# Two more weight units of the second tile loaded ahead of the expert gather, and TensorE one step further behind

## The reference

```
u = expert_u[idx]; v = expert_v[idx]           # 128 experts for each token, 1024 values each
act = gelu(einsum("td,ted->te", x, u))
y = einsum("te,ted->td", gate * act, v)
```

## Time and profile before

| | |
|---|---|
| median of 3 runs | 1198.71 us (1197.43 to 1200.72) |
| profiled execution | 1200.98 us, span 1199.2 us |
| TensorE busy | 881.1 us (73%) |
| VectorE busy | 815.8 us (68%) |
| ScalarE busy | 256.3 us (21%) |
| POOL busy | 319.6 us (27%) |
| moved by DMA | 402.51 MB, mean 336 GB/s |
| of it gathers and modulation chunks, queue q0 | 293.62 MB |
| of it weights and inputs, queue q1 | 105.62 MB |

### The profile page before, as it was taken

The page is one execution under the profiler, slowest core; times in us unless marked ns, Lnnn a source line. Parts: engine busy times, 40 slices in busy tenths (PEclk is TensorE's granted clock), DMA queues, the critical chain, the costliest instruction groups (busy, mean ns, idle before and its releaser), DMA issues. The chain is left out here.

```text
span 1199.2 us, 17385 instructions
## 1 busy us (share of the span) xinstructions
PE 881.1 (73%) x6808; PEld 667.9 (56%) x6808; DVE 815.8 (68%) x2091; ACT 256.3 (21%) x530; POOL 319.6 (27%) x284
## 2 busy tenths in 40 slices
PE   6999999886786895868444444444445499999998
PEld 6899697875675672745121111211212198888887
DVE  5666555687898767756798777777765689953411
ACT  2411111135222223121021011111100324143100
POOL 0001000142243333414555454544444100000000
PEclk9899999997898797987555555555556699999999
DMA  9977696799999999999999999999999845313230
GB/s 354 393 276 312 246 393 264 272 421 423 403 417 422 415 422 421 422 420 381 421 421 421 421 421 421 421 421 422 419 416 421 333 180 181 117 71 140 107 141 36
DMA packets 51554, 402.51 MB, mean 336 GB/s; under 512 B 5648, under 2 KB 7952, under 8 KB 9104
## 3 DMA queue, kind: packets, MB, share of 16 engines
q0 software_dynamic: 40320, 293.62, 59.7%
q1 hardware_dynamic: 10288, 105.62, 22.1%
q10 hardware_dynamic: 864, 2.16, 0.5%
HBM read 400.32 MB, written 1.05 MB: 335 GB/s over the span
## 5 line engine op out<-in xcount | busy, mean ns | idle before, releaser
L576 PE MATMUL ps<-arena 128*32 128x256 f32 x1536 | 161.4, 561 | 223.2 <-DVE arena L1540 223.1
L433 POOL DMA_INDIRECT arena<-uv_dram,arena x192 | 229.5, 1196 | 342.3 <-PE ps L576 270.9
L1522 DVE CUSTOM_DVE_ANT_0 arena<-arena 128x1024 f32<-128x1024 f32 x192 | 232.2, 1225 | 90.2 <-DMA arena<-uv_dram,arena 84.8
L576 PEld LDWEIGHTS ps<-arena 128*32 128x32 f32 x1536 | 52.6, 144 | 313.9 <-DVE arena L1540 266.5
L869 PE MATMUL ps<-xn,wring 128*128 128x256 f32 x576 | 125.0, 379 | 0.0
L1057 ACT ACTIVATE gel<-dots 128x2 f32<-128x2 f32 x128 | 26.0, 203 | 436.3 <-DVE dots L1522 401.7
L869 PEld LDWEIGHTS ps<-xn,wring 128*128 128x128 f32 x576 | 109.3, 190 | 14.8
L487 PE MATMUL ps<-xn,wring 128*128 128x128 f32 x896 | 113.0, 288 | 3.4 <-DMA wring<-units_dram 1.8
L487 PEld LDWEIGHTS ps<-xn,wring 128*128 128x128 f32 x896 | 109.5, 203 | 10.5 <-issue 6.5
L433 POOL DMA_INDIRECT wring<-uv_dram,arena x64 | 76.9, 1201 | 93.9 <-PE ps L576 83.8
L576 PE MATMUL ps<-wring,arena 128*32 128x256 f32 x512 | 51.3, 538 | 64.3 <-DVE arena L1540 64.3
(11 more groups left out here) (270 smaller groups left out, 1161.5 us busy)
## 6 DMA issues: line engine op xcount, KB each, us to landing
wring<-units_dram SPq DMA_DIRECT2D x46, 2048.0 KB, 10.0
arena<-mod_dram POOLq DMA_DIRECT2D x24, 1024.0 KB, 9.6
arena<-uv_dram,arena POOLq DMA_INDIRECT x192
wring<-units_dram SPq DMA_DIRECT2D x2, 1024.0 KB, 7.3
arena<-units_dram SPq DMA_DIRECT2D x1, 2048.0 KB, 8.9
hA<-x_t_dram SPq DMA_DIRECT2D x2, 512.0 KB, 7.8
arena<-mem_t_dram SPq DMA_DIRECT2D x1, 1024.0 KB, 9.6
arena<-keys_dram ACTq DMA_DIRECT2D x2, 512.0 KB, 6.9
```

Source lines behind the costliest of these rows:

```text
L433: pool.indirect_dma_start(ring[b], None, uv_d, bass.IndirectOffsetOnAxis(ap=idx[:, n:n + 1], axis=0)).then_inc(sem(f"row_in{b}"), 16)
L576: mm = pe.matmul(acc_ps(q)[G * c:G * (c + 1), :], lhsT=diag[:, s % 2, j, :], rhs=ring[b][:, D + 256 * c:D + 256 * (c + 1)], start=(p == 0 ...
L1522: post(V.tensor_tensor_reduce(out=ring[b][:, 0:D], in0=ring[b][:, 0:D], in1=x_rep[q % 2], scale=1.0, scalar=0.0, op0=ALU.mult, op1=ALU.add ...
```

## The change

The list of loads begins tile 1's units earlier and in another order: q, then tile 0's pq1, then b, v and k. q goes into a new buffer 4, the arena's first 4096 columns, which are two buffers of the gather's ring (now the ring's fifth and sixth, before its first and second) and which hold the memory tokens until the last mem_v unit of tile 0 is done. k goes into slot 2 of wring, which is also the ring's seventh and eighth buffer. So POOL's gather 4 waits for the pair of tile 1's q, and gather 6 for that of its k. From c on the loads alternate between slots 1 and 0 as before. Before, pq1, q and k of tile 1 were issued together and v waited for q's pair, b for k's.

TensorE gets its own distance: at point s it does slot s - 3 (PE_EARLY); VectorE and ScalarE stay at s - 2. Four semaphores are merged into others of the same engine.

```diff
+_first = [(1, "q"), (0, "pq1"), (1, "b"), (1, "v"), (1, "k")]
+_n = LOADS.index((0, "pq1"))
+LOADS[_n:_n + len(_first)] = _first
-LOAD_SLOT = ([i % 3 for i in range(len(CHAIN_UNITS[0]) - 1)] + [PQ1_SLOT] + [1 - i % 2 for i in range(len(CHAIN_UNITS[1]))]
+LOAD_SLOT = ([i % 3 for i in range(len(CHAIN_UNITS[0]) - 1)] + [4, PQ1_SLOT, 0, 1, 2] + [1 - i % 2 for i in range(len(CHAIN_UNITS[1]) - 4)]
...
+PE_EARLY = 3
...
-        ring = [area(2048 * b, 2048) for b in range(6)] + [wring[...] for i in range(2)]
+        ring = [area(2048 * b, 2048) for b in (2, 3, 4, 5, 0, 1)] + [wring[...] for i in range(2)]
...
-        w_pq1 = area(R, 4096).rearrange("p (k n) -> p k n", k=KB)
+        w_more = [area(a, 4096).rearrange("p (k n) -> p k n", k=KB) for a in (R, 0)]
...
+                elif (t, u) == (1, "q"):
+                    sp.wait_ge(sem("pairs"), PAIR_NO[0, "mem_v1b"] + 1)
...
+                elif n in (4, 6):
+                    pool.wait_ge(sem("pairs"), PAIR_NO[1, "q" if n == 4 else "k"] + 1)
...
-                if at[0] >= EARLY:
-                    slot(at[0] - EARLY)
+                if at[0] >= PE_EARLY:
+                    slot(at[0] - PE_EARLY)
...
-            for s in range(CHAIN_STEPS[1] - EARLY, SLOTS):
+            for s in range(CHAIN_STEPS[1] - PE_EARLY, SLOTS):
```

More of the change, by code:

```diff
@@ L205, in weights @@
             slot = LOAD_SLOT[LOAD_NO[t, u]]
-            return w_pq1 if slot == PQ1_SLOT else wring[:, slot]
+            return wring[:, slot] if slot < W_SLOTS else w_more[slot - W_SLOTS]
         def tokens(t):
             return slice(t * P, (t + 1) * P)
-        ring = [area(2048 * b, 2048) for b in range(6)] + [wring[:, 2, 4 * i:4 * i + 4, :].rearrange("p k n -> p (k n)") for i in range(2)]
+        ring = [area(2048 * b, 2048) for b in (2, 3, 4, 5, 0, 1)] + [wring[:, 2, 4 * i:4 * i + 4, :].rearrange("p k n -> p (k n)") for i in range(2)]
         mem_n = blocks(area(0, 2048), KB)
@@ L1324, in _ @@
             table(False)
-            go(act.activation(warm[:], cst("one"), ACT.Sigmoid), "warm")
+            go(act.activation(warm[:], cst("one"), ACT.Sigmoid), "act_step")
             gate_sigmoid(0)
@@ L1502, in modulation @@
                 dve.wait_ge(sem("mod_dot"), 2 * MOD_CHUNKS)
-                go(V.tensor_tensor(modc[:], modc[:], col("b_mod", 0, 48), ALU.add), "mod_read")
+                go(V.tensor_tensor(modc[:], modc[:], col("b_mod", 0, 48), ALU.add), "dve_step")
                 for layer in range(2):
@@ L1508, in modulation @@
                 go(V.tensor_tensor(gain2[:], col("norm_final", 0, KB), col("norm_final", 0, KB), ALU.mult))
-                go(V.tensor_scalar(gain2[:], gain2[:], EPS, None, ALU.add), "gain2")
-                go(V.memset(eps2[:], EPS * EPS), "gain2")
+                go(V.tensor_scalar(gain2[:], gain2[:], EPS, None, ALU.add), "dve_step")
+                go(V.memset(eps2[:], EPS * EPS), "dve_step")
                 go(V.tensor_tensor(gain_both[:], col("norm_final", 0, KB), gmod[:, 0], ALU.mult))
```

## The result

The changed kernel takes 1209.99 us (median of 4 runs, 1204.34 to 1215.7) against 1199.3 us: a ratio of 1.009, 95% interval 1.0063 to 1.0118. It is about 11 us slower, where 4.7 us less was forecast. The profiled execution took 1206.32 us (span 1204.5 us).

What follows compares the result with a forecast made beforehand. VectorE was taken to bound 240 to 350 us, transfers later; −1.7 − 2.2 − 1.8 + 1.0 = −4.7 us turned the profiled 1200.98 us into 1196.3 us, 1194.0 us from the median. Range 1187.5 to 1200.5 us.

Steps and rivals of the forecast that it cites:

- the price of the third step: At 405 to 450 us, rows given back 4.9 us later, less 3.9 us of vanished TensorE waits: +1.0 us, bounds +4.9 and −2.
- The term −2.2 (the squaring): Near 317.71 us, VectorE's wait for the chain's squaring goes because diag is ready: −2.2 us, bounds −4.4 and 0.
- the term −1.8 (the chain's end): At 536 to 556 us, TensorE finishes earlier, shortening VectorE's wait for unit pq1: −1.8 us, bounds −2.4 and 0.
- The loads go where room was: Before the first gather, q, b, v and k fit into nearly idle DMA time at 204 to 234 us: cost 0.
- POOL's two waits: Gathers 4 and 6 wait for q's and k's pairs yet land in time: taken 0, bound 0 to +2 us.
- The term **−1.7** for the bytes: In stage one, fewer bytes remove only VectorE's present wait for a row: −1.7 us, bounds −10 and 0.
- the 9.96 us: Transfer time at 421 GB/s of the two units, 4.19 MB together, no longer moved inside the gather.
- Neither sign of being wrong: Wrong if the stage to 350 us shortens by over 5 us, or VectorE waits for rows before 350 us.
- The rule weighed in the prediction: Work first on the busiest engine, here DMA; by it the change gives all 9.96 us. The waits at 245–350 us spoke against.
- slower: the ring is too short: Six rows in flight instead of eight, 4.9 us lost at each of the last two dips: +5.9 us, 1204.6 us, chance 0.11.
- All the bytes come back: Stage one's VectorE limit is really ordering that TensorE's earlier work loosens: −9.96 us, 1188.7 us, chance 0.15.
- It idles the DMA engines and saves nothing: First two gains come, later release costs 3 us, chain's end brings nothing: about −1 us, 1197.8 us, chance 0.27.

Runs made afterwards that it cites:

- the loads alone: Changed kernel with TensorE two steps behind again; moved loads, buffers and POOL's two waits stay: ratio 0.9977, 1195.33 us against 1198.27 us.
- The lag with the copies on time: Changed kernel, TensorE still three steps behind, but making the repeated products that ScalarE copies one slot earlier in slots 0 to 47: ratio 1.0053.
- six rows in flight: Kernel before, with POOL's gathers 6 to 105 also waiting until the row six gathers back is free: ratio 1.0162.
- the kernel with the lag up to step 6: Changed kernel with TensorE three steps behind only up to step 6, then two: ratio 0.9981.

## Why the prediction was wrong

The step that failed is **the price of the third step**: the term +1.0, with a bound of +4.9 us. It measured +14.3 us (after against the loads alone; 13.5 by the ratios), +15.3 us with the loads of before, and this includes whatever the two gains counted on below gave. Three things were wrong.

*The release was sized at the wrong place.* I took a half unit and a slot, 4.9 us, from the stretch of whole units. Where the chain's step ends in the chunk state products, TensorE's slot stands behind a wait for VectorE and 6.7 us of its own products (372.38 to 379.10 us), and the buffers come back 8.0 us later than before. It was looked for only at the dips that were there, and it made a new one, 286 GB/s at 376 to 404 us. The lag with the copies on time costs 8.0 us alone.

*A reader was left out.* TensorE's slot does more than free rows: its products for ScalarE's copies moved by a step too, and ScalarE stayed. The profile of before shows the margin, had I asked ScalarE for its waits: 15.7 us already, in five of these six copies. This costs 8.0 us alone, and no rival had it.

*Gains of the lag were counted as time.* The term −2.2 (the squaring) and the term −1.8 (the chain's end) name waits that did go: none for TensorE is left between 245 and 350 us, and at the chain's end the 5.19 us for pq1 are gone. But the gelu's waits came instead, 2.18 us at 321 us and 7.10 us at 535 us. Neither term is seen in the stage. The prediction's sentence that TensorE stood at each step for diag is also too strong: of the seven slots at 405 to 450 us in the kernel before, four waited, and without a wait there is nothing to gain.

The rest held. The loads go where room was; q left at 186.02 and k at 212.28 us, 8 us ahead of the forecast as gather 0 is. POOL's two waits cost nothing that lasts: slots 1 and 2 are 0.5 us behind, and from slot 3 to 18 the changed kernel is 0.3 to 1.6 us ahead of before (3.7 us at slot 11). The term **−1.7** for the bytes measured −1.8 us in the stage and −2.8 us by the ratio (0.8 to 4.7): the mechanism held, and the agreement to a tenth is luck. The rest of the 9.96 us became idle DMA engines, 86 × (413 − 373)/421 = 8.2 us at 234 to 320 us. Neither sign of being wrong came, since both look ahead of 350 us (VectorE waits 0.3 us for a row at 245 to 350 us), and the loss lies behind.

The rule weighed in the prediction, that of the Trainium skill (Perfetto Trace Analysis, Identifying the Most-Contended Engine) to work first on what is busiest, was put to two runs: with DMA engines full in both places, 8.7 us of bytes gave 0 before the dips and 8.4 us behind them. The trace agrees with the same page's Optimization Strategy, that the most contended engine changes over time.

Of the rivals, *slower: the ring is too short* (0.11, +5.9 us) had the first mechanism, rows held longer: six rows in flight cost 19.0 us, seven 6.7 us. It was priced too low and knew nothing of the second. *All the bytes come back* is out. *It idles the DMA engines and saves nothing* was right on the bytes only.

Open: whether the parts of the chain add up to the whole (10.0 against 14.3 us in the stage, 19.0 against 13.5 by the ratios), why the two causes together cost less than their sum, and what the weight loads that leave earlier beside the rows take, at slot 19 above all.

## What to carry to other kernels

When an engine's share of a shared step is moved, list everything that it hands on in that step, buffers and products alike, and ask every receiver for its present wait: one that already waits for it has no margin for more delay. Size the delay at the place where most stands between the old and the new position, not at a typical one. A present wait is a warning, not a price: taking it away gave nothing here, lengthening it cost 8.0 us. Bytes removed from a stretch were time here only where the reader waited for transfers before the next dip; the loads without the lag were the version worth keeping (0.9977).

## What the runs showed of the hardware

The same instructions ahead of the change took 8 us less in one execution. Windows of the kernel before, then of the changed one, at 20 to 60 us:

```profile
20.00:40.00 20.00, 18.18 (x146) 17.94 (x146) 14.76 (x42) 8.09 (x12) 2.33 (x4) 0.91 0.99 376
40.00:60.00 20.00, 17.46 (x117) 16.30 (x116) 13.31 (x39) 10.17 (x18) 0.00 (x0) 0.83 0.93 391
```

```profile
20.00:40.00 20.00, 19.17 (x165) 18.52 (x165) 16.35 (x49) 10.81 (x16) 2.32 (x4) 1.00 1.02 399
40.00:60.00 20.00, 17.47 (x149) 16.71 (x148) 15.86 (x37) 8.03 (x14) 0.53 (x1) 1.00 0.97 394
```

With a granted clock of 0.91 and 0.83, TensorE started 146 and 117 matmuls, with 1.00 in both 165 and 149. The 1.00 is the level of 2.4 GHz throughout, the others are windows in part at 1.2 GHz. The 16 products of one slot show the two levels: 1.07 us at 372.48 us before, 1.93 us at 379.10 us after. The clock is not all of the 8 us: the kernel with the lag up to step 6 had 0.91 and 1.00 here, and issued gather 0 at 232.16 us all the same. Over the sixteen profiled kernels gather 0 was issued between 224.85 and 233.62 us. So a median over few runs may carry several us that are not the kernel's: the changed kernel's four runs were 1204.34, 1206.32, 1213.65 and 1215.7 us.
